# Feed-forward rows transposed without the norm's factor, which is applied to gate sums and to the last product

## What is computed

```python
x = x + merged @ w_out
h2 = rms_norm(x, ffn_norm_gain)      # x * rsqrt(mean(x*x) + eps) * gain
gate, up = split(h2 @ w_gate_up)     # 2 x 2816 columns
x = x + (silu(gate) * up) @ w_down
return rms_norm(x, final_norm_gain)
```

## Time and profile before

| | |
|---|---|
| median of 3 runs | 907.86 us (907.37 to 908.78) |
| span of the profiled execution, first to last instruction | 906.1 us |
| PE busy | 887.1 us (98%) |
| DVE busy | 574.6 us (63%) |
| ACT busy | 438.6 us (48%) |
| POOL busy | 53.5 us (6%) |
| DMA engines, moved | 151.70 MB, mean 167 GB/s |

### The profile page before, as it was taken

How to read it: one execution, slowest core, us unless ns; L and a number is a source line. 1 busy time by engine, 2 the same in 40 slices (tenths; PEclk the granted TensorE clock), 3 DMA queues, 4 the chain that set the end, 5 groups by cost and what they waited for, 6 DMA issues and landing times.

```text
span 906.1 us, 14153 instructions
## 1 busy us (share of the span) xinstructions
PE 887.1 (98%) x5792; PEld 766.9 (85%) x5792; DVE 574.6 (63%) x880; ACT 438.6 (48%) x644; POOL 53.5 (6%) x79
## 2 busy tenths in 40 slices
PE   8999999999999999999989999899999999999996
PEld 6888999898999888888779999677888788888885
DVE  4975664574647665655569977654377667777543
ACT  6744444744344544444356524663444555555441
POOL 1000000000020110000110141100000100000000
PEclk9999999999999999999999999999999999999998
DMA  9657643455445545555656655004565555555441
GB/s 304 218 186 218 223 147 133 139 186 186 136 149 181 187 148 177 166 189 187 225 188 152 175 123 204 3 2 140 140 232 182 167 186 186 186 186 186 163 163 47
DMA packets 127799, 151.70 MB, mean 167 GB/s; under 512 B 16967, under 2 KB 93126, under 8 KB 127734
## 3 DMA queue, kind: packets, MB, share of 16 engines
q1 hardware_dynamic: 127594, 150.70, 51.9%
q0 software_dynamic: 64, 0.07, 0.0%
q10 hardware_dynamic: 76, 0.02, 0.0%
HBM read 148.67 MB, written 3.68 MB: 168 GB/s over the span
## 4 chain that ended last, share of the span: by engine, by line
PE 86%; DVE 7%; ACT 3%; issue 1%; DMA 1%; SPq 1%; POOL 1%; POOLq 0%; DVEq 0%; ACTq 0%
PE bank L513 17%; PE bank L515 17%; PE bank L514 17%; PE bank L1250 9%; PE bank L539 5%; PE bank L1238 5%; PE bank L540 2%; DVE w_lo L1954 2%; DVE arena L2331 1%; DMA arena<-in_mem 1%; ACT w_hi L1426 1%; PE bank L720 1%; PE bank L700 1%; PE bank L819 1%; PE bank L939 1%
## 5 line engine op out<-in xcount | busy, mean ns | idle before, releaser
L1954 DVE TENSOR_TENSOR w_lo<-ring,w_hi 128x2048 fp32r<-128x2048 f32 (+1 forms) x134 | 300.6, 2249 | 142.9 <-ACT w_hi L1426 142.2
L1426 ACT ACTIVATE w_hi<-ring 128x2048 fp32r<-128x2048 f32 (+1 forms) x134 | 250.3, 1871 | 129.4 <-PE bank L515 85.2
L513 PE MATMUL bank<-h_both,w_hi 128*128 128x256 f32 x496 | 143.1, 289 | 2.0 <-DVE w_lo L1954 2.0
L514 PE MATMUL bank<-h_both,w_hi 128*128 128x256 f32 x496 | 140.3, 283 | 0.0
L515 PE MATMUL bank<-h_both,w_lo 128*128 128x256 f32 x496 | 140.3, 283 | 0.0
L1250 PE MATMUL bank<-h_both,w_hi 128*128 128x512 f32 x352 | 123.4, 398 | 0.0
L513 PEld LDWEIGHTS bank<-h_both,w_hi 128*128 128x128 f32 x496 | 95.0, 192 | 4.2 <-DVE w_lo L1954 2.7
L1238 PE MATMUL bank<-h_both,w_lo 128*128 128x256 f32 x352 | 97.8, 281 | 0.4 <-ACT h_both L1449 0.4
L514 PEld LDWEIGHTS bank<-h_both,w_hi 128*128 128x128 f32 x496 | 95.1, 192 | 0.6 <-issue 0.5
L515 PEld LDWEIGHTS bank<-h_both,w_lo 128*128 128x128 f32 x496 | 95.1, 192 | 0.0
L513 PE MATMUL bank<-w_hi,h_both 128*128 128x512 f32 (+1 forms) x224 | 86.1, 384 | 0.0
(11 more groups left out here) (343 smaller groups left out, 1477.2 us busy)
## 6 DMA issues: line engine op xcount, KB each, us to landing
ring<-in_w_in SPq DMA_DIRECT2D x59, 1024.0 KB, 5.0
ring<-in_w_gate_up SPq DMA_DIRECT2D x44, 512.0 KB, 4.4
ring<-in_w_down SPq DMA_DIRECT2D x10, 1024.0 KB, 5.0
ring<-in_w_mem_kv SPq DMA_DIRECT2D x8, 1024.0 KB, 7.4
ring<-in_w_in SPq DMA_DIRECT2D x8, 512.0 KB, 5.0
ring<-in_w_gla_out SPq DMA_DIRECT2D x4, 1024.0 KB, 4.9
ring<-in_w_x_out SPq DMA_DIRECT2D x4, 1024.0 KB, 5.1
ring<-in_w_dsa_out SPq DMA_DIRECT2D x4, 1024.0 KB, 5.5
```

The costliest lines, as they stand in the source:

```text
L513: mm(o, ah, bh, start=start, stop=False, skip_group_check=True)
L514: mm(o, ah, bl, start=False, stop=False, skip_group_check=True)
L1426: act(w_hi[:, k % NHI, 0:m], ring[:, order.index(name) % NSLOT, 0:m], ACT.Copy)\
L1954: tt_(w_lo[:, i, 0:m], ring[:, i, 0:m], w_hi[:, k % NHI, 0:m].bitcast(F), ALU.subtract)\
```

## The change

The transposes read `xres` directly, so that `h_hi` and `h_lo` hold gain times row without the factor. In the loop, the gate sums are multiplied by the factors, laid out along tokens in `scale_row`, before tanh; the up sums stay without. The last add multiplies the down projection's bank by the factor of its token (line 2643 becomes a `scalar_tensor_tensor`). `scale_row` is made from two diagonal tiles (identity times factor, DVE) by one plain fp32 product with a column of ones (bank rb), after gu0a.

The transposes stand in three places: 8 (k 0 to 3) between the halves of w2o1b, 4 (k 4 to 7, first token tile) behind it, 4 (second tile) behind k = 0 of gu0. The two identity products are gone. In a block the order of the column groups is 0, 2, 3, 1. The bank of gu01 is opened without a wait; the wait for w2o11's reader, whose bank it is, stands ahead of its first product. DVE's remainder of gu0b's weights is moved behind the add of w2o11, ACT's rounding of Tf0 and Tf1 ahead of the squares of the second half. tanh and the two gate steps run once for 512 columns, no longer twice for 256.

Left out below are `high_of_transposed`, `low_of_transposed` and `tokens_part`'s caller, which get a list of columns or a `between` passed through.

```diff
--- before.py
+++ after.py
@@ -226,7 +226,8 @@
         f_hi, f_lo = (rounded(n, SPLIT + at, [128, FT, S]) for n, at in (("f_hi", second_at), ("f_lo", second_at + FT * S)))
         g_fin_at = second_at + 2 * FT * S
         f_spare_at = g_fin_at + D
-        assert f_spare_at + 1024 <= ARENA
+        f_scale_at = f_spare_at + 1024
+        assert f_scale_at + 512 <= ARENA
 
         ring = ctx.enter_context(nc.sbuf_tensor("ring", [128, NSLOT, 2048], F))
         ctx.enter_context(nc.sbuf_tensor("under_arena", [128, SPLIT - HI_AT], F))
@@ -333,6 +334,8 @@
         g_fin = flat(g_fin_at, D)
         gate_sum = [flat(probT_at + 256 * i, 256) for i in range(4)]
         up_sum = [flat(f_spare_at + 256 * i, 256) for i in range(4)]
+        gate_pair, up_pair = (tiled(at, 2, 512) for at in (probT_at, f_spare_at))
+        scale_diag, scale_row = tiled(f_scale_at, TT, 128), flat(f_scale_at + 256, S)
 
 
         w1, w2 = A["w_in"][0], A["w_in_2"][0]
@@ -465,11 +468,11 @@
         def _(pe):
             loads = [0] * NSLOT
 
-            def open_bank(name):
+            def open_bank(name, wait=True):
 
                 n = len(turns)
                 turns[name] = n
-                if n >= 8:
+                if n >= 8 and wait:
                     pe.wait_ge(bank_read[n % 8], n // 8)
                 return banks[n % 8]
 
@@ -599,7 +602,7 @@
                 last_rows()
                 tokens_part(f"{name}1", f"{name}1a", x, 0, 4, KT - 1)
                 tokens_part(f"{name}0", f"{name}0b", x, 4, 8, KT - 1, tag)
-                tokens_part(f"{name}1", f"{name}1b", x, 4, 8, KT - 1)
+                tokens_part(f"{name}1", f"{name}1b", x, 4, 8, KT - 1, between=between)
 
             def wide_tokens(title, x, between=None, tag=None):
 
@@ -1226,42 +1229,67 @@
             merge_part("bn", 1, (oT_hi, oT_lo), None, gdn_transposes)
             merge_part("bg", 0, (z2_hi, z2_lo), "z2_split")
             merge_part("bg", 1, (z2_hi, z2_lo), None, lambda: transpose_wide("2", ma, (0, 1)))
-            rows_projection("w2o", (m2_hi, m2_lo), "2", lambda: transpose_wide("2", ma, (2, 3)))
-            transpose_tokens("f", xn, 2)
+            def transpose_residual(t, columns):
+
+                for j in columns:
+                    for kk in range(2):
+                        k = 2 * j + kk
+                        ins = nc.tensor.transpose(bank_of(f"Tf{j}")[:, 256 * kk + 128 * t:256 * kk + 128 * t + 128],
+                                                  xres[:, t, 128 * k:128 * k + 128], ident)
+                    if t == TT - 1:
+                        done(f"Tf{j}", ins)
+
+            def residual_half():
+
+                for j in range(2):
+                    open_bank(f"Tf{j}")
+                for t in range(TT):
+                    pe.wait_ge(*read(f"w2o0{t}"))
+                    transpose_residual(t, (0, 1))
+
+            rows_projection("w2o", (m2_hi, m2_lo), "2", lambda: transpose_wide("2", ma, (2, 3)), residual_half)
+            for j in (2, 3):
+                open_bank(f"Tf{j}")
+            pe.wait_ge(*read("w2o10"))
+            transpose_residual(0, (2, 3))
+
+            def token_scales():
+
+                bank = open_bank("rb")
+                pe.wait_ge(signal("scale_diag"), 1)
+                done("rb", mm(bank[:, 0:256], const("ones").broadcast_to([128, 128]),
+                              scale_diag.rearrange("p a b -> p (a b)"), start=True, stop=True))
+
             def gate_up_part(j, half):
 
                 name, k0 = f"gu{j}{half}", 0 if half == "a" else 4
                 wh, wl = split_unit(name, 512)
-                early = range(2) if name == "gu0a" else ()
-
-                def low_weights(k, c, start, stop):
-                    return mm(bank_of(f"gu{j}{c}")[:, 0:256], wl[:, k - k0, 128 * c:128 * c + 128], h_hi[:, k, :],
-                              start=start, stop=stop, skip_group_check=True)
-
-                for k in early:
-                    pe.wait_ge(signal("high_f"), 1)
-                    for c in range(4):
-                        low_weights(k, c, k == 0, False)
                 for k in range(k0, k0 + 4):
                     if j == 0:
                         pe.wait_ge(*read(f"Tf{k // 2}"))
-                    for c in range(4):
+                    for c in (0, 2, 3, 1):
                         o, w = bank_of(f"gu{j}{c}"), slice(128 * c, 128 * c + 128)
-                        ins = mm(o[:, :], wh[:, k - k0, w], h_both[:, :, k, :], start=k == 0 and k not in early,
-                                 stop=False, skip_group_check=True)
-                        if k not in early:
-                            ins = low_weights(k, c, False, k == KT - 1)
+                        if j == 0 and k == 0 and c == 1:
+                            pe.wait_ge(*read("w2o11"))
+                        mm(o[:, :], wh[:, k - k0, w], h_both[:, :, k, :], start=k == 0, stop=False, skip_group_check=True)
+                        ins = mm(o[:, 0:256], wl[:, k - k0, w], h_hi[:, k, :], start=False, stop=k == KT - 1,
+                                 skip_group_check=True)
                         if k == KT - 1:
                             done(f"gu{j}{c}", ins)
+                    if j == 0 and k == 0:
+                        pe.wait_ge(*read("w2o11"))
+                        transpose_residual(1, (2, 3))
                 if half == "a":
                     part_done(name, ins)
                 else:
-                    unit_used[name] = full(f"gu{j}3")
+                    unit_used[name] = full(f"gu{j}1")
 
             for j in range(FT // 2):
                 for c in range(4):
-                    open_bank(f"gu{j}{c}")
+                    open_bank(f"gu{j}{c}", j > 0 or c != 1)
                 gate_up_part(j, "a")
+                if j == 0:
+                    token_scales()
                 gate_up_part(j, "b")
             for c in range(2):
                 for t in range(TT):
@@ -1375,14 +1403,14 @@
         tanh_users = [f"zx{j}" for j in range(4)] + [f"zg{j}" for j in range(4)] + [f"zd{j}" for j in range(4)]
         tanh_users += [f"bo{b}{c}{t}" for kind, b, c in merge_slots if kind == "bo" for t in range(TT)]
         tanh_users += [f"conv{j}" for j in range(6)] + ["z0", "z1"]
-        tanh_users += [f"gu{j}{t}" for j in range(FT // 2) for t in range(TT)]
+        tanh_users += [f"gu{j}" for j in range(FT // 2)]
 
         def tanh_read(name):
 
             if name.startswith("conv"):
                 return signal("silu_done"), int(name[4:]) + 1
             if name.startswith("gu"):
-                return signal("gated"), 2 * int(name[2:-1]) + int(name[-1]) + 1
+                return signal("gated"), int(name[2:]) + 1
             return read(name)
 
 
@@ -1801,26 +1829,27 @@
                     highs(splits_by[f"w2o{c}{t}"] + (3 if (c, t) == (0, 1) else 2))
                     sc.wait_ge(*read(f"w2o{c}{t}"))
                     half_squares("f", xres[:, t, 512 * c:512 * c + 512], 4, c, t)
-            high_of_transposed("f", h_hi)
+                high_of_transposed("f", h_hi, (2 * c, 2 * c + 1))
+            copy("rb", scale_row, bank_of("rb")[:, 0:256])
 
             def ffn_high(j):
-                sc.wait_ge(signal("gated"), 2 * j + 2)
+                sc.wait_ge(signal("gated"), j + 1)
                 act(pair(f_hi, j), prob[:, j % 2, :], ACT.Copy).then_inc(signal("f_high"), 1)
 
-            def low_tokens(name, dst, user):
+            def low_tokens(name, dst, j):
                 bank_ready(name)
-                if user >= 4:
-                    sc.wait_ge(signal("gated"), user - 3)
+                if j >= 2:
+                    sc.wait_ge(signal("gated"), j - 1)
                 act(dst, bank_of(name)[:, 256:512], ACT.Copy).then_inc(signal("low_tokens"), 1)
 
             for j in range(FT // 2):
                 for i in range(2):
-                    low_tokens(f"gu{j}{i}", gate_sum[(2 * j + i) % 4], 2 * j + i)
+                    low_tokens(f"gu{j}{2 * i}", (gate_sum, up_sum)[i][2 * (j % 2)], j)
                 if j > 0:
                     ffn_high(j - 1)
                 for i in range(2):
-                    low_tokens(f"gu{j}{2 + i}", up_sum[(2 * j + i) % 4], 2 * j + i)
-                    tanh(f"gu{j}{i}", gate_sum[(2 * j + i) % 4], wait=read(f"gu{j}{i}"), n=256)
+                    low_tokens(f"gu{j}{3 - 2 * i}", (up_sum, gate_sum)[i][2 * (j % 2) + 1], j)
+                tanh(f"gu{j}", gate_pair[:, j % 2, :], wait=(signal("gate_scaled"), j + 1))
             ffn_high(FT // 2 - 1)
             highs(len(splits))
             for c in range(2):
@@ -2590,15 +2619,23 @@
             low_of_rows("2", m2_lo, m2_hi, (2, 3))
             lows(splits_by["T23"] + 2)
             ve.wait_ge(signal("x_mid_back"), 16)
-            for c in range(2):
-                for t in range(TT):
-                    title = f"w2o{c}{t}"
-                    v = xres[:, t, 512 * c:512 * c + 512]
-                    bank_ready(title)
```

(59 more changed lines are left out.)

10 lines of the change are left out of this document (5 added, 5 removed).

## The result

| us | before | after |
|---|---|---|
| time, median (all runs) | 907.62 (907.05 to 908.78, 6 runs) | 901.45 (901.15 to 904.38, 6 runs) |
| ratio | 1 | 0.9932, 95% interval 0.992 to 0.9944 |
| span of the profiled execution | 906.1 | 899.7 (its time 901.48) |

The change gains 6.17 us, where 2.73 were forecast.

The account below looks back on a forecast made before the run. TensorE (PE), busy 98% of 906.1 us, was taken as the bound. 5.38 - 1.90 - 0.53 - 0.10 - 0.12 = 2.73 us off 907.86 gave 905.13; range 904.2 to 907.3.

Parts of the forecast that it names:

- the hole and its one-for-one gain: PE's gap without needed products, 708.66 to 714.04 us, goes; shortening it moves the end equally: 5.38 us.
- the transposes: Groups of 8, 4 and 4 between PE's other products cost 1.90 us, bounds 1.76 and 2.20.
- The two things that the Trainium skill: Around PE's transposes: lower clock (907.8) or a whole record, 0.274 us, per transpose (907.6); chance of the two 0.03.
- rb: Plain fp32 PE product in gu0 spreading the factors over the partitions: 0.53 us, bounds 0.43 and 0.86.
- the covers: Other engines' inputs reach PE in time behind the projection; thinnest is the add of w2o11, 0.67 us to spare.
- Rival 1: A cover fails (likeliest w2o11's add or gu00's bank) or the fp32 product costs double: 906.9 us, chance 0.14.
- rival 3: PE still waits for the factors, in the middle of gu0, so the hole only moves: about 907.5 us, chance 0.03.
- rival 4: The longer gate chain delays each block's weights in the loop, making the kernel slower: 910.7 us, chance 0.04.
- the wait on gu00's bank: At the end of gu0 PE waits once for DVE's first sum: 0.10 us, bounds 0 and 1.0.
- the dearer last adds: At the very end, two adds of wd1 with a scalar per partition lose 0.12 us, bounds 0 and 0.25.
- the block pace: In the gate/up loop PE keeps its steady pace, 0.3534 us a pair of products, so no gain there.
- the output: Behind DVE's last adds, the kernel's end stays unchanged apart from the dearer adds; no term was set for it.

Follow-up runs that it names:

- e8: Changed kernel with DVE's split of gu0b's weights put back ahead of the add of w2o11; 905.84 us, ratio 0.996.
- e12: Changed kernel with PE waiting at the start of each block after the first for the reader of the previous block's first bank; 906.57 us, ratio 0.9989.
- e5: Changed kernel run again, unaltered; 904.17 us, ratio 0.9945.
- e16: Changed kernel run a third time, unaltered; 904.97 us, ratio 0.9969.
- e1: Kernel before with only the loop's column-group order changed to 0, 2, 3, 1; 908.39 us, ratio 0.9997.
- e3: Kernel before with its weight order kept, but PSUM banks handed out as in the changed kernel; 907.95 us, ratio 0.9998.
- e4: Kernel before with weight columns in order 0, 2, 3, 1, but banks used one after the other; 907.79 us, ratio 0.9997.
- e7: Kernel before with one added PE wait, at the start of block 1, for the reader of gu00; 908.16 us, ratio 1.0004.
- e10: Kernel before without the eight low products that open the gate-and-up part, which stand at their own places instead; 909.41 us, ratio 1.0012.
- e15: Kernel before with PE waiting at the start of each block after the first for the reader of the previous block's first bank; 911.58 us, ratio 1.0038.
- e6: Changed kernel with the wait for gu00's bank moved from block 1's opening to the first product writing that bank; 902.39 us, ratio 0.9929.

## Why the prediction was right and wrong

**Right: the hole and its one-for-one gain.** The chain square, rsqrt, scaling left PE's path, and nothing took its place but what was listed: 2.79 us gained against 5.38 - 1.90 - 0.53 - 0.10 = 2.85.

**Right: the transposes.** 1.77 against 1.90, near the lower bound of 1.76; the row of eight between products priced them, not the length of one record. The two things that the Trainium skill (TensorE: Matmul & The Clock Gate, section Part 4: PE-mode transpose) made possible did not come: its 275 ns (for bf16) as a price each, an estimate by that page, would have shown as 2.2 us for the first group and it was 0.89, and the granted clock is 1.00 over the whole stretch. This row is of the kernel after:
```profile
705.00:717.00 12.00, 12.00 (x71) 10.45 (x70) 9.46 (x14) 7.81 (x18) 2.98 (x5) 1.00 0.63 205
```

**Right: rb and the covers.** rb cost 0.43 of 0.53: a weight read as one column 128 times costs what other fp32 weights do. DVE after:
```profile
709.29 0.69 DVE L2626 TENSOR_TENSOR arena<-arena,bank 128x512 f32<-128x512 f32 x1 [0.37 <-PE bank L518]
709.89 2.29 DVE L1983 TENSOR_TENSOR w_lo<-ring,w_hi 128x2048 fp32r<-128x2048 f32 x1
...
712.99 0.29 DVE L2636 TENSOR_SCALAR arena<-arena 128x128 f32<-128x128 f32 x1 [0.60 <-POOL arena L1884]
713.19 1.66 DVE L2023 SCALAR_TENSOR_TENSOR h_both<-bank,arena,h_both 128x256 fp32r<-128x256 f32 x4
```
The add of w2o11 ends at 709.98 and PE's product that needs it starts at 710.59: 0.61 us to spare, 0.67 forecast. The factors are there at 713.3 and rb starts at 715.55. Rival 1 and rival 3 did not happen, and in the loop the longer gate chain stayed off PE's path (no wait of PE but the one named), so rival 4 did not either.

**Mis-sized: the wait on gu00's bank**, 0.39 and not 0.10. By its own sign ("I am wrong if PE shows a wait ... on gu00's bank") the prediction was wrong here too. The order of events was as forecast. These are DVE's sums after, and the load of the weights (PEld) for PE's first product of block 1:
```profile
721.17 1.47 DVE L2647 TENSOR_TENSOR arena<-arena,bank 128x256 f32<-128x256 f32 x4 [0.48 <-ACT arena L1843]
```
```profile
721.82 0.19 PEld L1274 LDWEIGHTS bank<-h_both,w_hi 128*128 128x128 f32 x1 [0.45 <-issue]
```
The sum of gu00 is the first of the four, 0.42 us long by itself, so it ends at 721.59, 0.05 after PE's next product was due (721.42 + 0.12), and PE starts at 721.85, 0.26 after the read. The hand-over of 0.05 that I had assumed isn't the fault: in e8, where a single wait stands right ahead of the product, PE started 0.06 behind the end of DVE's add. What the sum left out are the waits in PE's queue behind the bank's: the trace has the bank's wait at 721.63, the one for the next weights at 721.74 and the weight load at 721.82. Where the stream doesn't stop, the same two waits are worked off 3 us ahead (729.92 and 730.03, for the block that starts at 733.02). The first stop of e12 has one wait more there and is 0.11 longer (0.544 for 0.435). The slower step after the restart, 0.07, was not in the sum either.

**Right: the dearer last adds**, 0.75 us each in place of 0.69, 0.13 against 0.12.

**Wrong: the block pace.** The step was "the pace inside the steady stretch as well. All that follows hangs on PE, so a shorter hole moves the end one for one", and "block pace 0.3534 a pair" as what the new profile would show. The one profile of before showed one pace, and I took it for the price of the products. It is one of two: 0.3533 or 0.3467, worth 2.1 us over ten blocks, settled where the stream restarts. The first profile after had the better one, which is 2.3 of the 3.4 us missing, and that five of the first six executions were of this kind was luck. Where most executions had the other pace the median was 904.2 and 905.0 (e5, e16), near the forecast of 905.1.

**Wrong by omission: the output.** The forecast carried what lies behind DVE's last product over unchanged. In it was an instruction fetch among the output's transfers, whose place hangs on the length of DVE's program; that it went gave 0.88 us. The profile of before shows the fetch only where the kinds of transfers in the last 4 us are looked at. Without it e5 and e16 would lie at 905.1 and 905.9.

**Chance: the clock ahead of the hole**, 0.48 us between the two profiles. The time around the span did not move: the forecast put 1.76 there, and the profiled execution after has 901.48 - 899.7 = 1.8.

**The range** was made of the bounds of the listed steps alone. Two things outside them, both on the gaining side, carried the time below 904.2. The sign and its chance (faster, 0.79) came out; the size was right for the hole only.

What stays open: what in TensorE makes the two cycles; why the kernel before fell into the dearer one at its first start in each of its seven profiles (before, e1, e3, e4, e7, e10, e15); and why the first six executions of the changed kernel were mostly the better ones.

## What to carry to other kernels

Taking a normalization factor off the path by scaling afterwards is worth the hole in TensorE's timeline, less the work put there, each price read from the same work in a like place between other products. Keep the engine's stream of products unbroken: a stop costs more than its length, because other waits in the engine's queue stand behind it (0.26 us here for a read that ended 0.05 late) and because the stream can come back at another pace. Moving a wait to the product that really needs it (e6) gave 1.8 us against the changed kernel beside it (902.4 against 904.2). When two versions differ by 2 us in 900, profile each more than once before explaining the difference, and look at what the queues carry in the last microseconds.
